# First weight block in halves, identity products ahead, earlier transposes and a tile buffer of its own in a one-layer decoder step

## What is computed

```python
def trunk_layer(x, ...):
    xn = rmsnorm(x, norm_attn)
    proj = xn @ w_in                   # q, k, v, gates of both branches
    h = mlstm_chunked(...)             # branch a: matrix memory, normalised
    branch_a = sigmoid(mo) * h
    branch_b = swa_prompt(...) or swa_sample(...)   # window 128, 16 heads, sinks
    merged = sigmoid(ga) * branch_a + sigmoid(gb) * branch_b
    x = x + merged @ w_out
    x = x + square(relu(rmsnorm(x, norm_mlp) @ w_up)) @ w_down
    return rmsnorm(x, norm_final)      # and the states and caches
```

## Time and profile before

| | us |
|---|---|
| median of 3 runs | 1740.41 |
| lowest, highest | 1738.8, 1741.91 |
| the profiled execution | 1738.82 |
| its span | 1737.1 |
| PE busy in it | 1706.4 (98%) |
| DVE, ACT, POOL busy | 787.8, 506.1, 104.5 |

### The profile page before, as it was taken

The page is one execution under the profiler, slowest core; times in us unless marked ns, Lnnn a source line. Parts: engine busy times, 40 slices in busy tenths (PEclk is TensorE's granted clock), DMA queues, the critical chain, the costliest instruction groups (busy, mean ns, idle before and its releaser), DMA issues.

```text
span 1737.1 us, 25882 instructions
## 1 busy us (share of the span) xinstructions
PE 1706.4 (98%) x10319; PEld 1558.2 (90%) x10319; DVE 787.8 (45%) x1513; ACT 506.1 (29%) x1189; POOL 104.5 (6%) x204
## 2 busy tenths in 40 slices
PE   7999999999999999999999999999999999999998
PEld 7999998999987898888999988899999988888996
DVE  5313333442155345673525445544444444455447
ACT  5423333232245333542303311122221211112222
POOL 3001101000011100120001000000000000000001
PEclk9999999999999999999999999999999999999999
DMA  6114353733121123111420111011110111110112
GB/s 210 51 42 126 56 85 71 86 55 55 34 49 25 44 43 71 25 25 35 142 61 25 49 49 49 25 48 48 48 48 31 41 48 48 48 42 31 48 61 103
DMA packets 140731, 99.24 MB, mean 57 GB/s; under 512 B 82456, under 2 KB 132640, under 8 KB 140648
## 3 DMA queue, kind: packets, MB, share of 16 engines
q1 hardware_dynamic: 140648, 98.08, 23.3%
HBM read 88.43 MB, written 11.60 MB: 58 GB/s over the span
## 4 chain that ended last, share of the span: by engine, by line
PE 98%; DVE 1%; ACT 1%; issue 0%; DMA 0%; POOL 0%; SPq 0%; POOLq 0%; ACTq 0%; DVEq 0%
PE bank L791 36%; PE bank L1154 22%; PE bank L1127 22%; PE bank L1113 6%; PE bank L753 3%; PE bank L946 2%; PE bank L975 2%; PE bank L856 1%; PE bank L848 1%; PE bank L851 1%; PE bank L893 1%; PE bank L831 0%; PE bank L875 0%; DMA xin<-in_x_prompt 0%; PE bank L1015 0%
## 5 line engine op out<-in xcount | busy, mean ns | idle before, releaser
L1974 DVE TENSOR_TENSOR x<-bank,x 128x512 f32<-128x512 f32 x288 | 195.7, 689 | 139.0 <-PE bank L1154 137.3
L1127 PE MATMUL bank<-xT_hi,w_hi 128*128 128x384 f32 (+1 forms) x768 | 250.5, 326 | 1.0 <-DVE xT_lo L1590 1.0
L1127 PE MATMUL bank<-xT_hi,w_lo 128*128 128x384 f32 (+1 forms) x768 | 250.4, 326 | 0.0
L1127 PE MATMUL bank<-xT_lo,w_hi 128*128 128x384 f32 (+1 forms) x768 | 250.3, 326 | 0.0
L1154 PE MATMUL bank<-w_hi,hid_hi 128*128 128x512 f32 x576 | 227.1, 394 | 0.0
L1154 PE MATMUL bank<-w_lo,hid_hi 128*128 128x512 f32 x576 | 226.1, 392 | 0.0
L1154 PE MATMUL bank<-w_hi,hid_lo 128*128 128x512 f32 x512 | 204.1, 399 | 0.0
L791 PE MATMUL bank<-xT_hi,w_hi 128*128 128x384 f32 (+1 forms) x1008 | 195.6, 335 | 0.0
L1525 ACT ACTIVATE relu<-bank 128x384 f32<-128x384 f32 (+1 forms) x96 | 45.5, 474 | 495.6 <-PE bank L1127 495.6
L791 PE MATMUL bank<-xT_hi,w_lo 128*128 128x384 f32 (+1 forms) x1008 | 186.3, 326 | 0.0
L791 PE MATMUL bank<-xT_lo,w_hi 128*128 128x384 f32 (+1 forms) x1008 | 186.1, 326 | 0.0
(11 more groups left out here) (206 smaller groups left out, 2191.3 us busy)
## 6 DMA issues: line engine op xcount, KB each, us to landing
raw<-in_w_in SPq DMA_DIRECT2D x64, 256.0 KB, 4.5
raw<-in_w_up SPq DMA_DIRECT2D x16, 1024.0 KB, 5.5
raw<-in_w_down SPq DMA_DIRECT2D x16, 1024.0 KB, 4.9
raw<-in_w_in SPq DMA_DIRECT2D x10, 1024.0 KB, 6.3
xin<-in_x_prompt SPq DMA_DIRECT2D x8, 512.0 KB, 4.3
bc<-gate_rows SPq DMA_DIRECT2D x32, 128.0 KB, 5.5
Cin<-in_state_C SPq DMA_DIRECT2D x4, 1024.0 KB, 8.3
out<-Cin SPq DMA_DIRECT2D x16, 256.0 KB
```

What stands on the lines that cost most here:

```text
L1127: last = nc.tensor.matmul(bank[n % 4][:, 0:cn], w[:, slot, k * WCOLS + tile * P:k * WCOLS + (tile + 1) * P], x[:, k, c0:c0 + cn], start=(s ...
L1974: nc.vector.tensor_tensor(v, bank[4 + d % 4][:, :], v, ALU.add).then_inc(free_v, 1)
```

## The change

It does eight things.

1. SP loads the value columns of block 0 in two halves (k 0 to 3, k 4 to 7), with tile 1 between them. The gate columns and the first half count on a semaphore of their own, `raw_first`.
2. ACT and DVE split block 0 in two halves of 1056 columns; the first goes ahead of tile 0's rounding and rest.
3. PE multiplies the identity with itself 14 times before the first transposes, into a bank that is free.
4. The transposes of tile 1 move from before unit 0 to between its second and third pass.
5. In `prompt`, attention units 14 and 15 are ordered like the others: transposes (and ACT's copy) before the filling.
6. `ss_outputs(7)` moves behind the first two score groups of `prompt(1)`; DVE copies the sampled queries before its first filling of `sampled`.
7. Tile 0 of the merged rows gets a buffer of its own, `xm` (rounded part and rest), so ACT and DVE write it before the last projection unit has been read.
8. The last output tile is scaled and stored in two halves of 512 columns.

```diff
@@ -101,6 +101,7 @@
 SPLIT_AT = 3
+WARM = 14
 NB = SEQ // P
@@ -311,6 +312,7 @@
             smask = a("smask", [P, MASKW])
+            xm = a("xm", [P, 2, KT, P], F32R)
             with ExitStack() as s2:
@@ -340,6 +342,8 @@
         raw_in = [sem(f"raw_in{n}") for n in range(2)]
+        raw_first = sem("raw_first")
+        w_first = sem("w_first")
         w_hi_done = sem("w_hi_done")
@@ -464,7 +468,7 @@
         RAW_DMAS = [{"aq": 4, "mo": 4, "ga": 4, "gb": 4, "out": 4}.get(x[0], 1) for x in BLOCKS]
-        RAW_DMAS[0] = 2
+        RAW_DMAS[0] = 1
         RAW_AT = [16 * sum(RAW_DMAS[b % 2:b + 1:2]) for b in range(B_MLP)]
@@ -513,8 +517,10 @@
                     sp.dma_start(r[:, :, 0:8], w_in_k[:, :, C_GATE:C_GATE + 8],
-                                 allow_slow_non_contiguous=True).then_inc(raw_in[b % 2], 16)
-                    sp.dma_start(r[:, :, 8:], w_in_k[:, :, C_MV:C_MV + DV]).then_inc(raw_in[b % 2], 16)
+                                 allow_slow_non_contiguous=True).then_inc(raw_first, 16)
+                    sp.dma_start(r[:, 0:KT // 2, 8:], w_in_k[:, 0:KT // 2, C_MV:C_MV + DV]).then_inc(raw_first, 16)
+                    load_x(1)
+                    sp.dma_start(r[:, KT // 2:, 8:], w_in_k[:, KT // 2:, C_MV:C_MV + DV]).then_inc(raw_in[b % 2], 16)
                 elif kind in ("v", "mk", "mq", "av", "ak"):
@@ -544,7 +550,6 @@
             sp.dma_start(gain_b[:, :], norm_attn[0].partition_broadcast(P)).then_inc(gain_in, 16)
-            load_x(1)
             load_block(0)
@@ -737,14 +742,19 @@
                          w_dn_k[:, 2 * (NG - 1):2 * NG, :]).then_inc(raw_in[1], 16)
-            for n, i in enumerate(DN_ORDER):
+            *sooner, i = DN_ORDER
+            for n, t in enumerate(sooner):
                 sp.wait_ge(y_rdy, n + 1)
-                sp.dma_start(y_rows(i), ybuf[0:rows_of(i), n % 2, :]).then_inc(y_out[n % 2], 16)
+                sp.dma_start(y_rows(t), ybuf[0:rows_of(t), n % 2, :]).then_inc(y_out[n % 2], 16)
+            for half in range(2):
+                at = slice(half * 512, half * 512 + 512)
+                sp.wait_ge(y_rdy, NT + half)
+                sp.dma_start(y_rows(i)[:, at], ybuf[:, (NT - 1) % 2, at]).then_inc(y_out[(NT - 1) % 2], 16)
             sp.wait_ge(pc_out, 64)
...
             sp.wait_ge(out_dma, 16 * (2 * NSEQ + 2 + 2 + 2 * NSEQ))
-            sp.wait_ge(y_out[0], 16 * ((NT + 1) // 2))
+            sp.wait_ge(y_out[0], 16 * ((NT + 1) // 2 + 1))
             sp.wait_ge(y_out[1], 16 * (NT // 2))
@@ -771,12 +781,18 @@
                 n = FIRST_UNIT[b] + u
+                if n == 0:
+                    pe.wait_ge(w_first, 1)
                 if BANK_BEFORE[n] is not None:
                     pe.wait_ge(free_a, BANK_BEFORE[n] + 1)
-                if u == 0:
+                if u == 0 and n:
                     pe.wait_ge(w_hi_done, b + 1)
...
                     (w, x), k = PASSES[step // KT], step % KT
+                    if n == 0 and step == KT // 2:
+                        pe.wait_ge(w_hi_done, 1)
+                    if n == 0 and step == 2 * KT:
+                        norm_transposes(1, xn)
                     if u == 0 and step == 2 * KT:
@@ -1029,16 +1045,15 @@
                 at_scores(u0 + 1)
+                if p:
+                    ss_outputs(NSEQ - 1)
                 fill(fills[0])
...
                         at_scores(u + 2)
-                        at_transposes(u)
-                        fill(fills[n + 1])
-                    else:
-                        fill(fills[n + 1])
-                        at_transposes(u)
+                    at_transposes(u)
+                    fill(fills[n + 1])
                     if n % 2:
@@ -1065,7 +1080,6 @@
                     ss_values(b)
-                ss_outputs(NSEQ - 1)
@@ -1080,8 +1094,9 @@
             pe.wait_ge(consts, 1)
+            for x in range(WARM):
+                nc.tensor.matmul(bank[3][:, 0:P], ident[:, :], ident[:, :], start=True, stop=True)
             norm_transposes(0, xn)
-            norm_transposes(1, xn)
             for u in range(NT):
@@ -1110,7 +1125,8 @@
                         for w, x in PASSES:
-                            last = nc.tensor.matmul(bank[m % out_ring(m)][0:rows_of(i), 0:WCOLS], x[:, k, cols(i)],
+                            lhsT = x[:, k, cols(i)] if i else xm[:, int(x is xT_lo), k, :]
+                            last = nc.tensor.matmul(bank[m % out_ring(m)][0:rows_of(i), 0:WCOLS], lhsT,
                                                     w_view(w, b, k), start=(step == 0), stop=(step == 3 * KT - 1))
@@ -1419,18 +1435,17 @@
                 u0 = p * HALF
+                if p:
+                    ss_out(NSEQ - 1)
                 at_exps(u0)
...
                     u = u0 + n
+                    at_copy(u)
                     if n + 2 < HALF:
-                        at_copy(u)
                         at_exps(u + 2)
-                        fill(fills[n + 1])
-                    else:
-                        fill(fills[n + 1])
-                        at_copy(u)
+                    fill(fills[n + 1])
                     if n % 2:
@@ -1451,7 +1466,6 @@
                     fill(fills[2 * b + 2])
-                ss_out(NSEQ - 1)
@@ -1459,9 +1473,12 @@
             square_x(0)
+            act.wait_ge(raw_first, 32)
+            nc.scalar.activation(w_hi[:, 0, part_cols(0, 0)], raw[:, 0, part_cols(0, 0)], ACT.Copy).then_inc(w_first, 1)
+            round_x(0)
             square_x(1)
-            round_x(0)
-            split(0)
+            act.wait_ge(raw_in[0], RAW_AT[0])
+            nc.scalar.activation(w_hi[:, 0, part_cols(0, 1)], raw[:, 0, part_cols(0, 1)], ACT.Copy).then_inc(w_hi_done, 1)
             square_x(2)
@@ -1486,10 +1503,11 @@
+            act.wait_ge(sg_use, len(GATES) - 2)
+            nc.scalar.activation(xm[:, 0, :, :], hT[:, :, cols(0)], ACT.Copy).then_inc(mg_hi, 1)
+            fill([last])
             act.wait_ge(gemm_a, PROJ_UNITS)
-            for i in range(NT):
-                if i == 1:
-                    fill([last])
+            for i in range(1, NT):
                 if i % 3 == 0:
@@ -1835,7 +1853,6 @@
             def sampled_dve(fills):
-                fill(fills[0])
                 dve.wait_ge(free_a, FIRST_UNIT[17])
@@ -1843,6 +1860,7 @@
                 ins.then_inc(ss_q, 1)
+                fill(fills[0])
                 ss_mask(0)
@@ -1879,9 +1897,15 @@
             norm_tile(0, xin[:, 0, :], xn)
+            dve.wait_ge(w_first, 1)
+            at = part_cols(0, 0)
+            nc.vector.tensor_tensor(w_lo[:, 0, at], raw[:, 0, at], w_hi[:, 0, at].bitcast(F32), ALU.subtract)
+            rest_x(0)
             norm_tile(1, xin[:, 1, :], xn)
-            rest_x(0)
-            split(0)
+            dve.wait_ge(w_hi_done, 1)
+            at = part_cols(0, 1)
+            nc.vector.tensor_tensor(w_lo[:, 0, at], raw[:, 0, at], w_hi[:, 0, at].bitcast(F32),
+                                    ALU.subtract).then_inc(w_lo_done, 1)
             norm_tile(2, xin[:, 2, :], xn)
@@ -1906,9 +1930,11 @@
-            for i in range(NT):
-                if i == 1:
-                    fill([last])
+            dve.wait_ge(mg_hi, 1)
+            nc.vector.tensor_tensor(xm[:, 1, :, :], hT[:, :, cols(0)], xm[:, 0, :, :].bitcast(F32),
+                                    ALU.subtract).then_inc(mg_lo, 1)
+            fill([last])
+            for i in range(1, NT):
                 dve.wait_ge(mg_hi, i + 1)
@@ -2001,7 +2027,15 @@
                         dve.wait_ge(y_out[n % 2], 16 * (n // 2))
-                normalise(2 * NT + n, x2[0:rows_of(i), i, :], ybuf, slot).then_inc(y_rdy, 1)
+                if n < NT - 1:
+                    normalise(2 * NT + n, x2[0:rows_of(i), i, :], ybuf, slot).then_inc(y_rdy, 1)
+                    return
+                dve.wait_ge(norm_rs, 3 * NT)
+                slot()
+                for half in range(2):
+                    at = slice(half * 512, half * 512 + 512)
+                    nc.vector.scalar_tensor_tensor(ybuf[:, n % 2, at], x2[:, i, at], rstd[:, 2, n:n + 1], gain_b[:, at],
+                                                   ALU.mult, ALU.mult).then_inc(y_rdy, 1)
```

## The result

The changed kernel takes 1729.55 us in the median of 5 runs (1729.12 to 1730.56), the kernel before 1741.91 (5 runs, 1738.8 to 1745.29; the three runs reported before the change are among them). The ratio is 0.9930, 95% interval 0.9917 to 0.9942. The forecast was 1730.7, range 1727.7 to 1734.3. The profiled execution took 1729.12 with a span of 1727.4: 9.7 less than before, the sum of the forecast.

A forecast was written before the change was run, and what follows sets the result against it. PE is busy for 98% of the span, so time can only be won where it stands still or works slowly. Terms 0.9 + 4.3 + 1.0 + 1.1 + 1.8 + 0.6 = 9.7; 1740.4 - 9.7 = 1730.7, range 1727.7 to 1734.3.

The forecast's parts named there:

- The two attention ends: Values at the end of attention in each half: waits of 2.19 and 2.43 for POOL shrink to 0.15; gain 4.3.
- The merge: PE's wait of 2.50 before the merged rows: with `xm` 0.7 stays, ended by DVE; gain 1.8, bounds 1.3 and 2.5.
- The rival by which waits come back a little further on: Middle of the kernel: ACT or DVE was pacing there anyway; gain 3, time 1737.4, chance 0.05.
- the one of the late weight halves: Start: the first weight half lands at 9.6 instead of 8.3; gain 8.4, time 1732.0, chance 0.04.
- The last sampled transpose: Sixteen score instructions (1.16) cover the 1.07 wait for DVE's gather; DVE's mask starts 0.6 earlier, early enough; gain 1.0.
- The start: Before unit 1: it starts at 18.0 instead of 18.86, DVE being late next; gain 0.9, bounds +1.3 to -2.6.
- That the clock holds: Start: PE keeps the fast pace through 2.8 idle before unit 0, as after 2.50 at the merge.
- One sign that the prediction had named for being wrong: Start: the first unit's products take 0.24 each; the forecast had eight products of unit 0 in about 1.1.
- The rival's unit 1 at 19.3: Start: the clock is low when unit 0 starts, so unit 1 begins at 19.3; gain 8.3, time 1732.1, chance 0.18.
- The tail: After the last product: storing in halves, the second issued about 0.1 later, gains 0.6, bounds -0.1 and 1.2.
- 1 left at both attention ends and at the merge: Rival of too short cover: POOL's selects or DVE's weight work stretch; gain 6.9, time 1733.5, chance 0.11.
- the cover check with a stretched select: Attention ends: 3.97 of cover against 3.8 of work, or 4.2 if POOL's select stretches to 1.31; 0 to 0.25 stays.

## Why the prediction was right, point by point

**The places in the middle.** The two attention ends gave 4.37 (forecast 4.3); the waits left are 0.0 and 0.23 (forecast 0.15 each). The first sampled scores gave 1.18 (1.1), late next was ACT's `kcT`, as named, with 0.58. The merge gave 1.88 (1.8), late next DVE's `xm` behind the weight rest, 0.62; moving that work took the rest away and so showed the cause. Undoing these parts brought each wait back in its old size. The rival by which waits come back a little further on is out, and so is the one of the late weight halves (8.24).

**The last sampled transpose** gave 1.08 (1.0), but not by its steps. At the place itself it was 1.27 (filling at 689.69 before, 684.38 after: 5.31 moved, against 4.04). Then 0.19 was given back: DVE's mask waits for that transpose, and its chain to `prob` ended at 689.96, just behind PE's arrival. "It was early enough" was wrong by that, and instead of no wait 0.18 was left at the transpose.

**The start** gave 0.75 (0.9). That DVE is late next was right for this execution, and undoing and filling showed it. That the clock holds was wrong: it fell, with a gap of 2.52 before unit 0. One sign that the prediction had named for being wrong so came true in part: eight products took 1.55 and then 1.97, not 1.1, and 1.97 is 0.24 to 0.25 each. That the number stood is luck in when the fall came. The rival's unit 1 at 19.3 (1.4 worse in all) is near what a sooner fall brings: 19.00 and 18.87 in two profiles with this start, with falls at 10.7 and 10.5, since there PE's slow work is the path, as the rival had it. In the changed kernel's own profile the fall came at 12.6 and DVE's work stood beside the slow stretch, which the rival left out. So the fall costs from next to nothing to 0.9. The Trainium skill (TensorE: Matmul & The Clock Gate, Part 1: The HAM clock gate) says of the rise to the fast pace that its point differs from run to run; these traces show the same of the fall. The identity products of the change bring nothing.

**The tail** gave 0.44 (0.6): the two issues landed 2.0 behind, as forecast, but the scaling in two pieces ends 0.13 later than in one (1.41 against 1.28). 2.6 - 2.0 - 0.13 = 0.47; the prediction had named both numbers and took 0.6 without subtracting the second.

**The sum** is 9.7 by forecast and 9.7 between the profiled spans; the errors of the terms (-0.15 at the start, -0.16 at the tail, -0.04 and +0.11 at the attention ends, +0.08 each at both sampled places and the merge) cancel. The agreement to a tenth is luck: the profiled execution is the shortest of the five, whose spans reach 1728.7.

**Sums beside it that don't come out.** The lower bounds of the parts add up to a gain of 2.5, not 2.1. With 1 left at both attention ends and at the merge the gain would be 7.7, not 6.9; with only the start, the tail and a third of the rest 4.2, not 3; and the cover check with a stretched select is 4.5 (3.8 + 1.31 - 0.64, the last being an unstretched select), not 4.2. At the second end the select did take 1.31, and 0.23 stayed, so that estimate was too high in its other parts. None of this enters the 9.7.

**From the span to the median** is the step that was mis-sized. The prediction carried the distance between median and profiled execution of the kernel before (1740.41 - 1738.82 = 1.6) over to the changed kernel. That distance was no constant of the measurement. It was, for the most part, a cost that went away when PE was kept busy in the four long waits, with the kernel before going down to 1738.96 without any work saved; clock falls behind such waits, seen in one trace, are the explanation that fits this and the mean clocks. In the changed kernel it went with the waits: its median is only 0.4 above its profiled execution, which makes 1729.5 where the prediction had 1730.7. For the kernel before the distance is itself uncertain, 1.6 in its first three runs and 3.1 in five (1741.91 - 1738.82); 3.1 - 0.4 is the 2.7 by which the medians moved further than the spans.

## What to carry to other kernels

Read a long wait of PE as its length plus a slow stretch that follows in some executions; a single profile may show none. Before pricing a slow clock, look at what runs beside PE there: where another engine is late next it costs only what it lasts beyond that engine's work, where PE is the bound it costs in full. And compare two orders only at a marker with the same work behind it.
